# Moving some SBUF arrays of a decoder-layer kernel by 64 bytes, so that every operand of its large products starts at 32 modulo 128

## The chip, the cores and the metric

The kernel runs on one NeuronCore of one Trainium2 chip. The metric is the device time of one execution in microseconds, less is better. Its engines are TensorE (PE, with the load of its stationary operand shown apart as PEld), VectorE (DVE), ScalarE (ACT), GpSimd (POOL) and SyncE (SP), which here only issues transfers.

## The reference

One decoder layer for 512 prompt tokens and 64 sample tokens, all in float32 with D = 2048. What is computed, cut down:

```python
def mixer_block(x, ...):
    h = rmsnorm(x, w_norm_mix)
    proj = h @ w_in                                  # 2048 x 6160
    o_r, s_ret = retention_chunkwise(...)            # 4 heads
    o_g, s_gla = gla_chunked(...)                    # 4 heads
    mix = concat(norm(o_r) * silu(g_r), norm(o_g) * silu(g_g))
    return x + mix @ w_out, s_ret, s_gla

def peer_block(x, ...):                              # 16384 experts, 16 of them for each of 8 heads
    h = rmsnorm(x, w_norm_ffn)
    q = (h @ w_pq).reshape(T, 8, 2, 128)
    s1, s2 = q[:, :, 0] . sub_keys1, q[:, :, 1] . sub_keys2
    eidx, gate = top 16 of the sums of the two top 16, softmax
    act = gelu(sum(u_tab[eidx] * h))
    return x + sum(gate * act * v_tab[eidx])

y = rmsnorm(peer_block(mixer_block(x)))
```

## The kernel before

The 576 tokens lie in five tiles (`PTILES` = 4 of 128 prompt tokens, one of 64 sample tokens). Every large product is done at about float32 accuracy with three products of type `float32r`: each operand is split in a high part (rounded by an ACT copy) and a low part (the rest, a DVE subtraction), and TensorE adds high·high, high·low and low·high in a PSUM bank. One such product is one PEld (128x128 stationary) and one matmul (384 or 512 columns of the moving operand).

The stages follow one another, with a barrier of all engines between them:

1. **in_proj** (`project`, blocks 0 to 2 of the input projection), 0 to 197 us. Stationary: the token rows `own_hi`, `own_lo`. Moving: 512 columns of the weights. A block of weights is four buffers `q` = 0 to 3, of which `q` = 1 and 2 are `own.whi`, `own.wlo` (which the trace calls `whi`, `wlo`) and `q` = 0 and 3 are `in_proj_whi`, `in_proj_wlo`, the projection's own arrays.
2. **mixer** (`project_and_mix`), to 867 us: the other blocks of the projection from `own` and `whi`, `wlo` (products L1600 to L1603), interleaved with the retention and GLA heads, whose small products use `mixer_*` arrays.
3. **out_proj**, to 1100 us, and **queries**, to 1323 us: `project` again, four blocks each (products L612, L617, L618; L612 and L615 for the sample tile). In queries the rows of tiles 1 to 3 are `dense_hi`, `dense_lo` (the "dense tokens", 384 of them), those of tiles 0 and 4 are `queries_rows_hi`, `queries_rows_lo`. Block 0 goes tile by tile with transposes (L601) between, blocks 1 to 3 without.
4. **hidden** (`experts_hidden`), to 2542 us: 128 units `n`, one for each 128 rows of `u_tab`. A unit is 48 products, its stationary `un.hi`, `un.lo` (the buffers `whi`, `wlo`), its moving operand `dense_hi`, `dense_lo`:

```python
for x in range(KT):
    mm(o, un.hi[s][:, x, :], h_hi[:, x, :], start=x == 0, stop=False)
    mm(o, un.hi[s][:, x, :], h_lo[:, x, :], start=False, stop=False)
un.ready(pe, n)
for x in range(KT):
    ins = mm(o, un.lo[s][:, x, :], h_hi[:, x, :], start=False, stop=x == KT - 1)
```

   Between units TensorE does small float32 products: in units 1 to 63 the scores of the router (whose top-16 search is DVE work, `route`), from unit 64 on the gate matrices (`hidden_tq`, L2058, 4 matmuls each, two or four groups of them in a unit). `un.ready` waits for the low part of the unit. DVE also takes one dot product for each gathered row (L2300).
5. **outputs** (`outputs`), to 3630 us: 128 units of 48 products, stationary `whi`, `wlo`, moving `outputs_w_hi`, `outputs_w_lo` (L2557 to L2559). Then **finish**.

SBUF arrays are laid out as a stack: `sbuf_tensor` puts the next array behind the last one from the low end, and with `side="right"` before the last one from the high end. So each array's start follows from the sizes of those that were put down before it. Starts modulo 128 bytes of the operands of the large products, worked out from those sizes, with the same number for every slice that a product takes, as all steps are multiples of 128 bytes:

| array | role | before | after |
|---|---|---|---|
| `whi`, `wlo` (shared) | stationary in hidden and outputs, moving elsewhere | 32 | 32 |
| `own_hi`, `own_lo`, `out_proj_rows_*`, `queries_rows_*` | stationary | 32 | 32 |
| `out_proj_whi`, `queries_whi` and their `wlo` | moving | 32 | 32 |
| `outputs_w_hi`, `outputs_w_lo` | moving | 32 | 32 |
| `in_proj_whi`, `in_proj_wlo` (q = 0, 3) | moving | 96 | 32 |
| `dense_hi`, `dense_lo` | stationary in queries, moving in hidden | 96 | 32 |
| `mixer_qk`, `_v`, `_kd`, `_qkT`, `_qd`, `_at`, `_S`, `_qm`, `_km`, `_dec` | small products of the mixer | 96 | 32 |
| `mixer_wa2`, `mixer_alr` | small products of the mixer | 64 | 0 |

Of the kernel before, what the change touches and what calls it, by code (L numbers as in the profile page):

```python
# [26 lines left out]
F32 = mybir.dt.float32  # L27
# [6 lines left out]
P = 128  # L34
# [4 lines left out]
TILES = SEQ // P + 1  # L39
# [42 lines left out]
class Steps:  # L82


    def __init__(self, eng, sem):
        self.eng, self.sem, self.base, self.n, self.offset = eng, sem, 0, 0, 0
# [25 lines left out]
class Alloc:  # L112
# [12 lines left out]
    def sb(self, name, shape, dt=F32):  # L125
        return self.ctx.enter_context(self.nc.sbuf_tensor(f"{self.name}_{name}", shape, dt))
# [542 lines left out]
class InputRows:  # L669


    def __init__(self, a, sb, whi, wlo):
        self.hi, self.lo = (sb(f"own_{p}", [P, KT, cols], F32R) for p, cols in (("hi", TP), ("lo", SEQ)))
        self.whi, self.wlo = whi, wlo
        self.rstd = sb("own_rstd", [P, 16])[:, 0:TILES]
        self.raw_in = [a.sem(f"own_raw_in{s}") for s in range(2)]
        self.hi_done, self.lo_done = a.sem("own_hi_done"), a.sem("own_lo_done")

# [1981 lines left out]
def build(nc, x, w, consts, keys, tables, states, outs):  # L2660

    def scratch(name, shape):
        return nc.dram_tensor(name, shape, F32, kind="Internal").ap()

    proj, alr = scratch("proj", (TP, PROJ - 2 * H * DV)), scratch("alr", (RANK, SEQ + NSMP))
    normed = scratch("normed", (TP, D))
    mix, sums = scratch("mix", (TP, D)), scratch("sums", (TP, D))
    queries, h_rows = scratch("queries", (TP, D)), scratch("h_rows", (2, P, D))
    hidden, G = scratch("hidden", (NCH, P, CH, ND)), scratch("gate_mat", (NCH, P, NG, CH, GT))

    with ExitStack() as ctx:
        def sb(name, shape, dt=F32, on=ctx):
            return on.enter_context(nc.sbuf_tensor(name, shape, dt))

        ident, squares = sb("ident", [P, P]), sb("squares", [P, D // NB, TILES])
        rstd_all = sb("rstd_all", [P, 16])[:, 0:TILES]
        shared = Alloc(nc, ctx, "units")
        raw = [sb(f"raw{s}", [P, KT // KQ, NB]) for s in range(2)]
        whi, wlo = ([sb(f"{name}{s}", [P, KT // KQ, NB], F32R) for s in range(2)] for name in ("whi", "wlo"))
        un = Units(nc, shared, raw, whi, wlo)  # L2680
        with ExitStack() as early:
            tiles = [sb(f"x{s}", [P, D], F32, early) for s in range(2)]
            held, ahead = (Held(shared, name, raw, whi, wlo, tiles) for name in ("held", "ahead"))
            with ExitStack() as inputs:
                own = InputRows(shared, lambda name, shape, dt=F32: sb(name, shape, dt, inputs), whi, wlo)
                project(nc, "in_proj", ident, consts["ident"], x, w["in"], proj, w_col_dram=w["norm_mix"], late=True,
                        small=(w["alr"], alr), own=own, held=held)
                project_and_mix(nc, "mixer", consts, ident, own, held, w["in"], w["out"], proj, alr, w["a2"], w["gn"], states,
                                outs["states"], normed, mix)
            project(nc, "out_proj", ident, None, mix, w["out"], sums, squares=squares, residual=x, first=True, held=held,  # L2690
                    then=(ahead, w["pq"]), rstd_all=rstd_all)
            expert_ids, gates0, dots = (ctx.enter_context(nc.sbuf_tensor(name, [P, NGATHER], dt, side="right"))
                                        for name, dt in (("expert_ids", U32), ("gates0", F32), ("dots", F32)))
            rows = ctx.enter_context(ExitStack())
            dense = [rows.enter_context(nc.sbuf_tensor(f"dense_{p}", [P, KT, ND], F32R, side="right")) for p in ("hi", "lo")]
            project(nc, "queries", ident, None, sums, w["pq"], queries, w_col_dram=w["norm_ffn_cols"], squares=squares, row=h_rows,
                    dense=dense, first=True, held=ahead, rstd_all=rstd_all, un=un, u_units=tables["u_units"])
        with rows:
            big, w_in = [shared.sb(f"big{n}", [P, NKEYS * GT]) for n in range(2)], shared.sem("w_in")
            experts_hidden(nc, "hidden", consts, ident, un, big, w_in, tables["u_units"], tables["v_units"], *dense, hidden, queries, keys, tables["u_rows"], h_rows,  # L2700
                           w["norm_ffn"], expert_ids, dots, gates0, G)
        acc, accg = sb("acc", [P, KT, ND]), [sb(f"accg{x}", [P, D]) for x in range(2)]
        X, early = sb("sums1", [P, D]), shared.sem("sums_early")
        outputs(nc, "outputs", un, big, w_in, tables["v_units"], hidden, G, tables["v_rows"], expert_ids, dots, acc, accg, sums, X, early)
        finish(nc, "finish", ident, sums, w["norm_final"], acc, accg, X, outs["y"])
# [62 lines left out]
```

## Time and profile before

| | |
|---|---|
| median of 3 runs | 3663.56 us (3657.59 to 3664.55) |
| profiled execution | 3668.83 us, its span 3667.0 us |
| PE, DVE, ACT, POOL busy | 3528.2, 2585.5, 1314.1, 937.1 us |
| granted TensorE clock, mean | 0.984 |

The span is the time from the first to the last instruction in the profiled execution; busy is the time in which an engine worked. Matmuls overlap, so the duration of one (334 ns) says little of the rate: that is read from the distance between the starts of consecutive ones, called pitch below.

### The profile page before, as it was taken

How to read it: one execution, taken by the hardware profiler on the slowest of the kernel's cores; microseconds unless marked ns; L12 is line 12 of the kernel's file. 1: busy time of each engine (PE TensorE's matmuls, PEld its weight loads, DVE VectorE, ACT ScalarE, POOL GpSimd, SP SyncE). 2: the span in 40 equal slices, each digit the busy share in tenths (PEclk: the TensorE clock that was granted, in tenths of full speed). 3: DMA queues.
4: the chain of work that ended last, by engine and by line, in shares of the span. 5: the costliest groups of instructions: out<-in, count | busy, mean ns of one | idle time of the engine just before them, and what ended most of it. 6: DMA issues, size and time to landing. Idle time of an engine off the chain costs nothing. (4 is left out here: it accounts for less than half of the span.)

```text
span 3667.0 us, 50045 instructions
## 1 busy us (share of the span) xinstructions
PE 3528.2 (96%) x19463; PEld 3267.5 (89%) x19463; DVE 2585.5 (71%) x3886; ACT 1314.1 (36%) x1671; POOL 937.1 (26%) x619
## 2 busy tenths in 40 slices
PE   8999999998989999999999999998999999999996
PEld 6877777776867889999999999998999999999996
DVE  4135555553224238999998888886898898998997
ACT  5111134442223223332236767673222222222222
POOL 0000000000000000233333333331555554554552
PEclk9999999999999999999999999999999999999998
DMA  5145343435334244688789999998989999989896
GB/s 204 50 144 172 108 140 128 125 130 185 141 107 162 86 156 160 256 329 333 293 321 364 384 376 375 382 374 343 360 339 372 360 356 377 360 355 370 348 359 243
DMA packets 193659, 965.07 MB, mean 263 GB/s; under 512 B 19697, under 2 KB 67121, under 8 KB 92706
## 3 DMA queue, kind: packets, MB, share of 16 engines
q1 hardware_dynamic: 121010, 516.50, 37.9%
q0 software_dynamic: 61424, 426.27, 29.9%
q10 hardware_dynamic: 11008, 19.26, 1.5%
q8 instruction: 154, 2.52, 0.3%
q14 instruction: 63, 0.52, 0.0%
HBM read 865.58 MB, written 96.37 MB: 262 GB/s over the span
## 5 line engine op out<-in xcount | busy, mean ns | idle before, releaser
L2068 PE MATMUL hidden_hp<-dense_hi,whi 128*128 128x384 f32 x2048 | 699.8, 342 | 6.1 <-PEq L123 6.1
L1836 ACT CAST whi<-raw 128x2048 fp32r<-128x2048 f32 x214 | 410.7, 1919 | 790.5 <-PE outputs_vp L2559 599.9
L2069 PE MATMUL hidden_hp<-dense_lo,whi 128*128 128x384 f32 x2048 | 691.8, 338 | 0.0
L2557 PE MATMUL outputs_vp<-outputs_w_hi,whi 128*128 128x384 f32 x2032 | 679.6, 334 | 3.3 <-DVE wlo L1840 3.1
L2559 PE MATMUL outputs_vp<-outputs_w_hi,wlo 128*128 128x384 f32 x2032 | 678.8, 334 | 0.0
L2558 PE MATMUL outputs_vp<-outputs_w_lo,whi 128*128 128x384 f32 x2032 | 678.7, 334 | 0.0
L2015 POOL DMA_INDIRECT hidden_row<-u_rows,expert_ids x192 | 363.5, 1893 | 1000.4 <-DVE dots L2300 625.4
L1840 DVE TENSOR_TENSOR wlo<-raw,whi 128x2048 fp32r<-128x2048 f32 x214 | 490.2, 2291 | 105.0 <-ACT whi L1836 103.4
L2493 DVE SCALAR_TENSOR_TENSOR accg<-outputs_row,outputs_w_op,accg 128x2048 f32<-128x2048 f32 x192 | 450.7, 2347 | 54.8 <-DMA outputs_row<-v_rows,outputs_id 51.8
L2300 DVE CUSTOM_DVE_ANT_0 hidden_row<-hidden_row,hidden_h_row 128x2048 f32<-128x2048 f32 x192 | 436.0, 2287 | 67.7 <-DMA hidden_row<-u_rows,expert_ids 64.8
L2355 POOL DMA_INDIRECT outputs_row<-v_rows,outputs_id x192 | 325.6, 1696 | 522.3 <-DVE accg L2493 477.8
L2068 PEld LDWEIGHTS hidden_hp<-dense_hi,whi 128*128 128x128 f32 x2048 | 386.6, 189 | 6.5 <-issue 6.5
L2072 PE MATMUL hidden_hp<-dense_hi,wlo 128*128 128x384 f32 x2048 | 380.1, 337 | 12.7 <-DVE wlo L1840 12.5
L2557 PEld LDWEIGHTS outputs_vp<-outputs_w_hi,whi 128*128 128x128 f32 x2032 | 381.4, 188 | 5.6 <-DVE wlo L1840 5.6
L2069 PEld LDWEIGHTS hidden_hp<-dense_lo,whi 128*128 128x128 f32 x2048 | 386.2, 189 | 0.0
L2558 PEld LDWEIGHTS outputs_vp<-outputs_w_lo,whi 128*128 128x128 f32 x2032 | 381.4, 188 | 0.0
L2559 PEld LDWEIGHTS outputs_vp<-outputs_w_hi,wlo 128*128 128x128 f32 x2032 | 381.4, 188 | 0.0
L2072 PEld LDWEIGHTS hidden_hp<-dense_hi,wlo 128*128 128x128 f32 x2048 | 359.2, 188 | 15.9 <-DVE wlo L1840 15.9
L1600 PE MATMUL mixer_acc<-whi,own_hi 128*128 128x512 f32 x720 | 297.8, 414 | 7.1 <-PEq L123 7.1
L1601 PE MATMUL mixer_acc<-wlo,own_hi 128*128 128x512 f32 x720 | 284.6, 395 | 0.0
L2146 ACT ACTIVATE hidden_hid<-hidden_hp 128x384 f32<-128x384 f32 x128 | 62.8, 491 | 571.7 <-PE hidden_hp L2072 571.7
L2347 POOL COPY outputs_id<-expert_ids 128x1 uint32 (+1 forms) x192 | 220.3, 1148 | 37.1 <-POOLq L123 35.9
(397 smaller groups left out, 5032.6 us busy)
## 6 DMA issues: line engine op xcount, KB each, us to landing
raw<-v_units SPq DMA_DIRECT2D x128, 1024.0 KB
raw<-u_units SPq DMA_DIRECT2D x86, 1024.0 KB
raw<-w_in SPq DMA_DIRECT2D x42, 1024.0 KB, 5.8
hidden_raw<-u_units SPq DMA_DIRECT2D x42, 1024.0 KB
hidden<-hidden_hid SPq DMA_DIRECT2D x128, 192.0 KB
gate_mat<-units_big SPq DMA_DIRECT2D x12, 2048.0 KB, 20.0
units_big<-hidden SPq DMA_DIRECT2D x16, 1536.0 KB
units_big<-gate_mat SPq DMA_DIRECT2D x16, 1536.0 KB
```

Source lines behind the costliest of these rows:

```text
L1836: self.nc.scalar.copy(self.hi[s][:], self.raw[raw][:]).then_inc(self.hi_done, 1)
L1840: self.nc.vector.tensor_tensor(self.lo[s][:], self.raw[self.slot(n, s)][:], self.hi[s][:].bitcast(F32), ALU.subtract).then_inc(self.lo_don ...
L2015: pool.indirect_dma_start(row[g % U_ROWS][:], None, u_rows, bass.IndirectOffsetOnAxis(expert_ids[:, g:g + 1], 0)).then_inc(row_in[g % U_RO ...
L2068: mm(o, un.hi[s][:, x, :], h_hi[:, x, :], start=x == 0, stop=False)
L2069: mm(o, un.hi[s][:, x, :], h_lo[:, x, :], start=False, stop=False)
L2072: ins = mm(o, un.lo[s][:, x, :], h_hi[:, x, :], start=False, stop=x == KT - 1)
L2300: v.tensor_tensor_reduce(r[:], r[:], h_row[g % 3 // 2][:], 1.0, 0.0, mult, ALU.add, dots[:, g:g + 1]).then_inc(row_used, 1)
L2355: pool.indirect_dma_start(self.row[j % ROWS][:], None, self.table, bass.IndirectOffsetOnAxis(self.id[j][:], 0)).then_inc(self.row_in[j % R ...
L2493: v.scalar_tensor_tensor(o[:], r[:], w_op[:, j:j + 1], o[:], mult, ALU.add).then_inc(gat.row_used, 1)
L2557: mm(o, un.hi[x][:, at, :], W_hi[s][:, e, :], start=e == 0, stop=False)
L2558: mm(o, un.hi[x][:, at, :], W_lo[s][:, e, :], start=False, stop=False)
L2559: ins = mm(o, un.lo[x][:, at, :], W_hi[s][:, e, :], start=False, stop=e == CH - 1)
```

## The change

Two arrays of 64 bytes per partition are added, neither of which is read or written. `own_rstd` grows from 16 to 32 floats (five are used), which moves all that is put down behind it in the stages in_proj and mixer up by 64 bytes. `edge` is put down from the high end before `expert_ids`, `gates0`, `dots`, `dense_hi` and `dense_lo`, which moves these five down by 64 bytes. No instruction is added, removed or moved on any engine.

```diff
@@ InputRows.__init__ @@
         self.hi, self.lo = (sb(f"own_{p}", [P, KT, cols], F32R) for p, cols in (("hi", TP), ("lo", SEQ)))
         self.whi, self.wlo = whi, wlo
-        self.rstd = sb("own_rstd", [P, 16])[:, 0:TILES]
+        self.rstd = sb("own_rstd", [P, 32])[:, 0:TILES]
@@ build @@
             project(nc, "out_proj", ident, None, mix, w["out"], sums, squares=squares, residual=x, first=True, held=held,
                     then=(ahead, w["pq"]), rstd_all=rstd_all)
+            ctx.enter_context(nc.sbuf_tensor("edge", [P, 16], F32, side="right"))
             expert_ids, gates0, dots = (ctx.enter_context(nc.sbuf_tensor(name, [P, NGATHER], dt, side="right"))
```

## Rows read from the trace of the kernel before

**Rows 1.** Busy time of each engine by stretch: columns named in the first row
```profile
core 0: us, PE busy (x) PEld busy (x) DVE busy (x) ACT busy (x) POOL busy (x), PEclk, DMA share, GB/s
1493.00:1896.00 403.00, 390.32 (x2263) 386.81 (x2263) 386.32 (x841) 118.88 (x118) 138.77 (x68) 1.00 0.82 315
1981.00:2433.00 452.00, 450.28 (x2775) 449.21 (x2774) 379.94 (x530) 316.15 (x547) 163.35 (x90) 1.00 0.99 380
2720.00:3635.00 915.00, 910.99 (x5262) 909.06 (x5261) 820.19 (x634) 246.70 (x139) 462.50 (x320) 1.00 0.90 353
```

**Rows 2.** Waits of PE, 1493 to 1900 us: total us, times, longest
```profile
PE hidden_hp L2072 <- DVE wlo L1840: 12.5, 8, 2.4
```

**Rows 3.** Waits of PE, 1981 to 2433 us
```profile
PE hidden_tq L2058 <- DVE hidden_spare L2308: 1.6, 1, 1.6
```

**Rows 4.** Waits of DVE, 1493 to 1900 us
```profile
DVE hidden_row L2300 <- DMA hidden_row<-u_rows,expert_ids: 7.2, 5, 2.5
DVE wlo L1840 <- ACT whi L1836: 0.2, 1, 0.2
```

**Rows 5.** Timeline of PE in outputs: start us, us, what
```profile
2999.77 0.33 PE L2557 MATMUL outputs_vp<-outputs_w_hi,whi 128*128 128x384 f32 x1
...
3002.89 0.33 PE L2557 MATMUL outputs_vp<-outputs_w_hi,whi 128*128 128x384 f32 x1
```

**Rows 6.** Timeline of PE in queries, block 2, tiles 0 and 1
```profile
1240.45 0.39 PE L612 MATMUL queries_acc<-queries_whi,queries_rows_hi 128*128 128x512 f32 x1
...
1243.17 0.39 PE L612 MATMUL queries_acc<-queries_whi,dense_hi 128*128 128x512 f32 x1
...
1249.35 0.39 PE L612 MATMUL queries_acc<-queries_whi,dense_hi 128*128 128x512 f32 x1
```

**Rows 7.** Timeline of PE in in_proj: `in_proj_whi`, then `whi`
```profile
80.35 0.39 PE L612 MATMUL in_proj_acc<-in_proj_whi,own_hi 128*128 128x512 f32 x1
...
85.84 0.39 PE L612 MATMUL in_proj_acc<-in_proj_whi,own_hi 128*128 128x512 f32 x1
...
109.98 0.39 PE L612 MATMUL in_proj_acc<-whi,own_hi 128*128 128x512 f32 x1
...
112.02 0.39 PE L612 MATMUL in_proj_acc<-whi,own_hi 128*128 128x512 f32 x1
```

**Rows 8.** Timeline of PE in hidden: the 16 last products of five units
```profile
1840.91 2.94 PE L2072 MATMUL hidden_hp<-dense_hi,wlo 128*128 128x384 f32 x16
...
1997.92 2.99 PE L2072 MATMUL hidden_hp<-dense_hi,wlo 128*128 128x384 f32 x16
...
2428.32 2.99 PE L2072 MATMUL hidden_hp<-dense_hi,wlo 128*128 128x384 f32 x16
...
2496.92 2.96 PE L2072 MATMUL hidden_hp<-dense_hi,wlo 128*128 128x384 f32 x16
...
2530.45 2.96 PE L2072 MATMUL hidden_hp<-dense_hi,wlo 128*128 128x384 f32 x16
```

**Rows 9.** Timeline of PE, units 67 and 100 of hidden: start, end of each
```profile
1942.80 0.42 PE L2068 MATMUL hidden_hp<-dense_hi,whi 128*128 128x384 f32 x1
...
1951.20 1.05 PE L2058 MATMUL hidden_tq<-hidden_spare 128*128 128x128 f32 x8
...
2272.94 0.42 PE L2068 MATMUL hidden_hp<-dense_hi,whi 128*128 128x384 f32 x1
...
2281.51 1.95 PE L2058 MATMUL hidden_tq<-hidden_spare 128*128 128x128 f32 x16
```

**Rows 10.** Timeline of PE in outputs behind two waits
```profile
2718.39 0.44 PE L2557 MATMUL outputs_vp<-outputs_w_hi,whi 128*128 128x384 f32 x1 [2.08 <-DVE wlo L1840]
...
2720.24 0.33 PE L2558 MATMUL outputs_vp<-outputs_w_lo,whi 128*128 128x384 f32 x1
...
2852.99 0.45 PE L2557 MATMUL outputs_vp<-outputs_w_hi,whi 128*128 128x384 f32 x1
...
2854.86 0.33 PE L2558 MATMUL outputs_vp<-outputs_w_lo,whi 128*128 128x384 f32 x1
```

**Rows 11.** Timeline of DVE around 2196 us: a gathered row that came late
```profile
2196.26 2.29 DVE L2300 CUSTOM_DVE_ANT_0 hidden_row<-hidden_row,hidden_h_row 128x2048 f32<-128x2048 f32 x1 [4.80 <-DMA hidden_row<-u_rows,expert_ids]
```

## The prediction, made before the changed kernel was run

> **What bounds the kernel now.** I read the stretches first, then the waits of PE and of DVE, then PE's timeline in each stage, looking at the pitch of consecutive products. The reader is to see in the stretches that PE is busy nearly all the time in every part but one. From 1981 to 2433 us it is busy 450.3 of 452 us, in outputs 911.0 of 915 us [rows 1]. There the pitch of the products is the time. The exception is 1493 to 1896 us, where the router runs. PE waits there eight times, 12.5 us in all, for the low part that DVE makes [rows 2]. DVE itself is busy 386.3 of 403 us [rows 1], and of the rest it waits 7.2 us for gathered rows and only 0.2 us for anything that hangs on PE [rows 4]. In that stretch DVE with its gathers sets the pace.
>
> So the question is whether the pitch depends on where the operands lie. This trace holds both cases.
>
> - **512 columns.** In queries, 12 pitches with the stationary operand in `queries_rows_*` (32 modulo 128) take 1243.17 − 1240.45 = 2.72 us, 226.7 ns each. At 1243.17 us the stationary goes over to `dense_*` (96), while the moving operand, the shape and the loop stay. The next 27 take 1249.35 − 1243.17 = 6.18 us, 228.9 ns each [rows 6]. In in_proj, 24 pitches with the moving operand at 96 take 5.49 us, 228.8 ns each, and 9 with it at 32 take 2.04 us, 226.7 ns [rows 7]. A pair that lies apart by 64 costs 2.2 ns more, whichever of the two it is.
> - **384 columns.** In outputs all lie at 32, and 18 pitches take 3.12 us, 173.3 ns each [rows 5]. In hidden, where the moving operand is at 96, units come in three kinds, told apart by the row of their 16 last products: 2.94, 2.96 or 2.99 us [rows 8]. Fifteen pitches lie in such a row, and the last matmul is some 0.335 to 0.34 us. So the pitches are about 173.3, 174.7 and 176.7 ns. A unit keeps its kind from its start to its end.
>
> **The change part by part.** No instruction changes, so all rests on the pitch, and on what else could depend on a start.
>
> *Hidden, 1981 to 2433 us.* Here 38 of the 44 units from 72 to 115 are of the 2.99 kind, the first and the last of them at 1997.92 and 2428.32 us [rows 8]. Unit 100 is one: its 48 pitches, from its first product to the first gate product behind it, take 2281.51 − 2272.94 = 8.57 us [rows 9]. 48 at 173.3 ns are 8.32 us. The 0.25 us above has two parts: the other pitches are 3.4 ns too long, 0.15 us, and 0.10 us are the restart. An aligned unit would not reach 8.32 us either, since it starts behind the gate products too. Two restarts in outputs show what aligned operands cost there: 10 pitches take 1.85 and 1.87 us in place of 1.733, that is 0.117 and 0.137 us more, after which the pitch is at 173.3 ns again [rows 10]. I take 0.125 us. The gain is 0.25 − 0.125 = 0.125 us for a unit, for 38 of them 4.75 us. Bounds: 0.113 and 0.133 us by the two restarts, so 4.3 to 5.1 us; nothing if the pitch hangs on something else.
>
> *Hidden, the other units behind the router.* The last six units follow one another without a restart and are of the 2.96 kind. The rows of five of them stand 2530.45 − 2496.92 = 33.53 us apart, 8.38 us for a unit against 8.32 [rows 8], so they give 0.4 us. About 15 more, of the 2.94 and 2.96 kinds, start behind gate products. Unit 67, of the first kind, takes 1951.20 − 1942.80 = 8.40 us [rows 9], 0.08 us above 8.32; the other kind has 1.3 ns more in each pitch, so 0.14 us. They lie on both sides of the aligned 0.125. Together I put −0.1 us on them. That makes 5.0 us.
>
> *Hidden, under the router.* Until 1896 us the gain of PE turns into a longer wait for DVE. I take 0 for 1493 to 1896 us, and 0.3 us for the units before, of which two are of the slowest kind. If all passed through, the some 45 units would give about 1.5 us: that is the upper end.
>
> *Queries.* Blocks 1 to 3 hold 3 x 3 tiles x 48 = 432 products on `dense_*` at 2.2 ns: 1.0 us. In block 0 every 12 products are interrupted by transposes, and the start costs as much as the pitch would give; I take 0.
>
> *In_proj.* Blocks 1 and 2 hold 2 x 2 buffers x (4 tiles x 12 + 8) = 224 products on `in_proj_whi`, `in_proj_wlo`: 0.5 us.
>
> *Mixer.* The large products keep their operands at 32. The small ones move from 96 to 32, and restart the large ones as before. No row shows a pair of them in both places. I take 0, with 1.5 us on either side: a hundred or so restarts with at most 10 to 15 ns, half the spread between the restarts in outputs [rows 10].
>
> *Outputs, finish.* No operand moves. They start earlier by what is gained before, since a barrier stands ahead of each stage. DVE, ACT and transfers keep their lengths: a start goes from 96 to 32 modulo 128, or from 64 to 0, and no row gives one of them another length for that.
>
> The sum is 4.75 + 0.25 + 0.3 + 1.0 + 0.5 = 6.8 us. The profiled execution took 3668.8 us (span 3667.0), so it would take 3662.0. Against the median of the runs, 5.3 us below it, the same difference gives 3663.6 − 6.8 = **3656.8 us**.
>
> **A rule that speaks against the change.** The rows of queries show two pitches for two places of one operand, with all else equal [rows 6]. The Trainium skill, "TensorE: Matmul & The Clock Gate", section "Step-by-step: what each phase is for", says that TensorE has two independent SBUF read ports, one for the streaming operand and one for the weight load, so that loading the next weights takes no read bandwidth from the running matmul. By that rule where the two lie to each other would not matter, and the sum would be 0 in place of 6.8 us. It is the first rival below.
>
> **The rivals.**
>
> - *The place isn't the cause: the pitch hangs on how a run of products starts.* For it: in hidden units of all three kinds read the very same arrays [rows 8], so the place alone can't set the kind; the phase at the restart must have a part. Against it: in queries the pitch changes at 1243.17 us in the middle of a run, with no restart [rows 6], and both restarts in outputs come back to 173.3 ns [rows 10]. If it holds, the units may fall into other kinds, and nothing is gained on the whole: 3663.6 us, give or take 3.
> - *The pitch falls, but the stretch behind it absorbs the gain.* From 1981 to 2433 us the DMA engines are busy at a share of 0.99 [rows 1]. For it: one row came 4.8 us late there [rows 11], and PE waited 1.6 us for DVE behind it [rows 3]. Against it: that is PE's only wait in 452 us, and in the fastest units the same share was no hindrance. Then only queries, in_proj and the last units are left: 1.0 + 0.5 + 0.4 + 0.3 = 2.2 us, so 3661.4 us.
> - *More is gained:* part of the 1.5 us under the router, the mixer's 1.5 us, and restarts as good as the best in hidden (0.08 us in place of 0.125, 38 x 0.045 = 1.7 us). 6.8 + 4.4 = 11.2 us: 3652.4 us.
> - *Slower: gathered rows come late more often.* A unit shorter by 1.2% asks for 1.2% more transfers per us, of engines that are busy at 0.99. Each late row like that in [rows 11] costs PE 1.6 us [rows 3]. It decides once there are more than four of them beside the present one, which eats the 6.8 us; with ten, the time is 3663.6 − 6.8 + 16 = 3672.8 us. Against it: every such wait also gives the transfers time to catch up, so the rate would settle where PE no longer gains, not beyond.
>
> **How the numbers follow.** A measurement of this kernel tells apart some 0.2%, 7.3 us: its three runs lie within 7 us. My forecast (gain of 4.5 to 9 us, 3654.5 to 3659) gets 0.53. No effect of the place gets 0.18, the absorbed gain 0.10, the larger gain 0.13, slower 0.06. The forecast lies just inside 7.3 us, so of its 0.53 I give 0.22 to faster; with the 0.13 and some 0.03 of the no-effect case faster is 0.38. Slower is 0.06 and 0.01 of no-effect, the rest, 0.55, is within 0.2%. The range reaches from the larger gain to no effect: 3652 to 3664 us.
>
> **What would show it.** Right: the rows of 16 products in hidden from 1981 us on are 2.93 to 2.94 us, none of 2.99; the pitch on `dense_*` in queries and on `in_proj_whi` is 226.7 ns; the stretch of units 72 to 115 is shorter by 4 to 5 us; 1493 to 1896 us keeps its length, with more of PE's wait on `wlo`; outputs keeps its own. Wrong: rows of 2.96 and 2.99 us with all operands at 32, PE waits on L2308 or on `whi` behind late transfers from 1981 us on, or a mixer that is longer by more than 2 us.

## The result and the profile after: 3675.6 us, slower by 0.28%

| | before | after |
|---|---|---|
| median (lowest to highest) | 3664.06 us of 10 runs (3657.59 to 3669.15) | 3675.64 us of 10 runs (3668.26 to 3677.64) |
| ratio, 95% interval | | 1.0028 [1.0019, 1.0038] |
| profiled execution, its span | 3668.83, 3667.0 us | 3675.49, 3673.7 us |
| PE busy | 3528.2 us | 3537.8 us |

The forecast was 3656.8 us, with a range of 3652 to 3664, so a kernel that is 6.8 us faster. It became slower by 7 to 14 us.

From the page of the changed kernel, PE's busy time and the three groups of hidden (busy us, mean ns of one):

```profile
PE 3537.8 (96%) x19463; PEld 3274.5 (89%) x19463; DVE 2585.6 (70%) x3886; ACT 1314.1 (36%) x1671; POOL 963.9 (26%) x619
...
L2068 PE MATMUL hidden_hp<-dense_hi,whi 128*128 128x384 f32 x2048 | 701.5, 343 | 6.1 <-PEq L123 6.1
L2069 PE MATMUL hidden_hp<-dense_lo,whi 128*128 128x384 f32 x2048 | 693.6, 339 | 0.0
...
L2072 PE MATMUL hidden_hp<-dense_hi,wlo 128*128 128x384 f32 x2048 | 382.1, 338 | 9.6 <-DVE wlo L1840 9.5
```

The same lines of before have 699.8, 691.8 and 380.1 us. DVE and ACT, whose operands moved too, are as busy as they were. The products themselves became longer. The stretches of the changed kernel, which answer to [rows 1]:

```profile
core 0: us, PE busy (x) PEld busy (x) DVE busy (x) ACT busy (x) POOL busy (x), PEclk, DMA share, GB/s
1493.00:1896.00 403.00, 394.52 (x2270) 391.63 (x2269) 385.42 (x838) 123.00 (x123) 137.05 (x67) 1.00 0.83 317
1981.00:2433.00 452.00, 451.16 (x2784) 450.86 (x2783) 383.46 (x529) 317.37 (x550) 172.40 (x92) 1.00 0.99 381
2720.00:3635.00 915.00, 910.70 (x5242) 908.01 (x5240) 820.66 (x630) 243.03 (x135) 474.86 (x322) 1.00 0.90 354
```

PE's waits in 1493 to 1900 us of the changed kernel, as in [rows 2] (us in total, times, longest):

```profile
PE hidden_hp L2072 <- DVE wlo L1840: 8.4, 7, 1.9
```

and in 1981 to 2433 us, as in [rows 3]:

```profile
PE hidden_tq L2058 <- DVE hidden_spare L2308: 0.8, 1, 0.8
```

Under the router PE waits 4.1 us less than in [rows 2] and is busy 4.2 us more: longer products use up a wait, they don't lengthen the stretch. Behind it nothing is late. So the pitch has to be looked at. PE in queries, block 2: a pair with `queries_rows_*`, the first one with `dense_*`, and the one behind the last (start us, us), as in [rows 6]:

```profile
1246.16 0.39 PE L617 MATMUL queries_acc<-queries_wlo,queries_rows_hi 128*128 128x512 f32 x1
...
1248.43 0.40 PE L618 MATMUL queries_acc<-queries_whi,queries_rows_lo 128*128 128x512 f32 x1
1248.66 0.40 PE L612 MATMUL queries_acc<-queries_whi,dense_hi 128*128 128x512 f32 x1
...
1257.03 0.39 PE L612 MATMUL queries_acc<-queries_whi,queries_rows_hi 128*128 128x512 f32 x1
```

10 pitches with `queries_rows_*` take 2.27 us, 227 ns each. The 36 with `dense_*` take 8.37 us, **232.5 ns** each, where before had 228.9. Both arrays, `queries_rows_*` and `dense_*`, now start at 32 modulo 128. In in_proj 24 pitches on `in_proj_whi`, `in_proj_wlo` take 5.60 us, 233.3 ns, where [rows 7] have 228.8:

```profile
80.01 0.39 PE L612 MATMUL in_proj_acc<-in_proj_whi,own_hi 128*128 128x512 f32 x1
...
85.61 0.39 PE L612 MATMUL in_proj_acc<-in_proj_whi,own_hi 128*128 128x512 f32 x1
```

In hidden, rows of 16 last products as in [rows 8]:

```profile
1984.60 2.98 PE L2072 MATMUL hidden_hp<-dense_hi,wlo 128*128 128x384 f32 x16
...
2224.12 2.98 PE L2072 MATMUL hidden_hp<-dense_hi,wlo 128*128 128x384 f32 x16
...
2535.51 2.98 PE L2072 MATMUL hidden_hp<-dense_hi,wlo 128*128 128x384 f32 x16
```

All rows of 16 from 1981 to 2433 us, 45 of them, say 2.98: a pitch of some 176 ns, between the second and the third kind of before. No unit is of the 2.94 kind any more. Outputs, whose operands didn't move, has 18 pitches in 3.12 us, as in [rows 5]:

```profile
2999.59 0.33 PE L2557 MATMUL outputs_vp<-outputs_w_hi,whi 128*128 128x384 f32 x1
...
3002.71 0.33 PE L2557 MATMUL outputs_vp<-outputs_w_hi,whi 128*128 128x384 f32 x1
```

### The profile page after: what moved, and what is told of

The parts are those of the page before. It is cut to its first block and busy times, and to the rows that moved or that the text cites. A ratio compares the mean times of both kernels' runs of the same rounds, so it can differ in the third digit from the quotient of the medians.

```text
span 3673.7 us, 50045 instructions
## 1 busy us (share of the span) xinstructions
PE 3537.8 (96%) x19463; PEld 3274.5 (89%) x19463; DVE 2585.6 (70%) x3886; ACT 1314.1 (36%) x1671; POOL 963.9 (26%) x619
## 5 line engine op out<-in xcount | busy, mean ns | idle before, releaser
L2068 PE MATMUL hidden_hp<-dense_hi,whi 128*128 128x384 f32 x2048 | 701.5, 343 | 6.1 <-PEq L123 6.1
L2069 PE MATMUL hidden_hp<-dense_lo,whi 128*128 128x384 f32 x2048 | 693.6, 339 | 0.0
L2015 POOL DMA_INDIRECT hidden_row<-u_rows,expert_ids x192 | 377.2, 1965 | 990.2 <-DVE dots L2300 602.4
L2068 PEld LDWEIGHTS hidden_hp<-dense_hi,whi 128*128 128x128 f32 x2048 | 386.4, 189 | 6.5 <-issue 6.5
L2072 PE MATMUL hidden_hp<-dense_hi,wlo 128*128 128x384 f32 x2048 | 382.1, 338 | 9.6 <-DVE wlo L1840 9.5
L2069 PEld LDWEIGHTS hidden_hp<-dense_lo,whi 128*128 128x128 f32 x2048 | 386.5, 189 | 0.0
L2072 PEld LDWEIGHTS hidden_hp<-dense_hi,wlo 128*128 128x128 f32 x2048 | 361.3, 188 | 12.5 <-DVE wlo L1840 12.5
L2347 POOL COPY outputs_id<-expert_ids 128x1 uint32 (+1 forms) x192 | 228.2, 1189 | 34.1 <-POOLq L123 32.9
```

The lines of the kernel that those rows point to most:

```text
L2015: pool.indirect_dma_start(row[g % U_ROWS][:], None, u_rows, bass.IndirectOffsetOnAxis(expert_ids[:, g:g + 1], 0)).then_inc(row_in[g % U_RO ...
```

## What the table of starts had left out

The table ahead of the prediction goes by 128 bytes. Worked out modulo 256 from the same sizes, the starts are:

| array | before | after |
|---|---|---|
| `whi`, `wlo`, `own_*`, `queries_rows_*`, `queries_whi`, `out_proj_*`, `outputs_w_*` | 32 | 32 |
| `in_proj_whi`, `in_proj_wlo` | 96 | 160 |
| `dense_hi`, `dense_lo` | 224 | 160 |

So 64 bytes carried each of the moved arrays not onto the others, but to the opposite side of a circle of 256. Below, *d* is the start of the moving operand less that of the stationary one, modulo 256. In queries and in_proj (512 columns) d was 64 and became 128. In hidden (384 columns), where `dense_*` is the moving operand, it was 192 and became 128. Outputs and out_proj have 0. In in_proj *d* follows from the size of `own_rstd` alone; in queries it also hangs on where the low and the high end of the memory lie. The table below checks this: at equal *d* the two stages agree within 0.7 ns in every kernel.

**Theory A:** the pitch hangs on d, it is shortest at 0, and 128 is worse than 64. **Rival B:** the absolute start counts (32 modulo 256 is the good one, 160 a bad one). **Rival C:** the places don't matter, and the kinds of the units are drawn anew in each execution. **Rival D:** something else that was moved (small products of the mixer, gathers, DVE) costs the time.

## The experiments

The edits are to the kernel before. `own_rstd` sets the place of `in_proj_w*` and the mixer's arrays, `edge` that of `dense_*`. All kernels compute all of the reference. `before` ran again beside each, and the ratios are to these runs: median 3665.29 us (29 runs, 3657.2 to 3675.78) beside all_256, all_256_up and edge_only, 3666.58 us (23 runs) beside rstd_only and after_again. A kernel of which there is one run has only its pitches to show, as single runs of before lie up to 19 us apart.

Means over whole stages, from the starts of all consecutive products (queries blocks 1 to 3 on `dense_*`; in_proj blocks 1 and 2 on `in_proj_w*`; hidden without waits and restarts), in ns:

| kernel | d in queries, in_proj, hidden | queries | in_proj | hidden |
|---|---|---|---|---|
| before | 64, 64, 192 | 229.0 | 229.0 | 175.0 |
| the same, again | 64, 64, 192 | 229.0 | 229.0 | 174.3 |
| after | 128, 128, 128 | 232.4 | 233.1 | 175.9 |
| the same, again | 128, 128, 128 | 232.4 | 232.9 | 175.9 |
| edge_only | 128, 64, 128 | 232.4 | 229.0 | 175.9 |
| rstd_only | 64, 128, 192 | 229.0 | 232.9 | 174.2 |
| all_256 | 0, 0, 0 | 226.7 | 226.8 | 173.4 |
| all_256_up | 0, 0, 0 | 226.7 | 226.8 | 173.4 |
| dist_96 | 96, 96, 160 | 233.4 | 233.4 | 173.3 |
| dist_160 | 160, 160, 96 | 234.2 | 234.3 | 176.6 |
| dist_192 | 192, 192, 64 | 233.4 | 233.3 | 173.3 |
| dist_224 | 224, 224, 32 | 233.2 | 233.3 | 174.1 |
| dist_320 | 64, 64, 192 | 229.0 | 229.1 | 174.3 |

Lengths of stages, from first product to first product, in us (the mixer, in_proj, out_proj and queries to their last product):

| stage | before | again | after | again | all_256 |
|---|---|---|---|---|---|
| in_proj | 181.10 | 181.04 | 181.94 | 181.97 | 180.40 |
| mixer | 646.18 | 643.31 | 649.48 | 641.72 | 646.85 |
| out_proj | 212.14 | 212.15 | 212.09 | 212.67 | 212.08 |
| queries | 216.53 | 216.67 | 218.45 | 219.56 | 215.60 |
| hidden, units 0 to 17 | 170.18 | 170.16 | 171.58 | 171.72 | 169.73 |
| 18 to 62 (router) | 402.78 | 404.67 | 402.90 | 403.35 | 403.71 |
| 63 to 71 | 95.86 | 92.33 | 94.34 | 95.84 | 94.57 |
| 72 to 115 | 440.93 | 433.72 | 438.83 | 437.76 | 434.22 |
| 116 to 126 | 100.16 | 101.03 | 101.04 | 101.05 | 99.66 |

### All operands at one place modulo 256

```diff
-        self.rstd = sb("own_rstd", [P, 16])[:, 0:TILES]
+        self.rstd = sb("own_rstd", [P, 64])[:, 0:TILES]
...
+            ctx.enter_context(nc.sbuf_tensor("edge", [P, 48], F32, side="right"))
```

> own_rstd has 64 floats and edge 48, so the moving and the stationary operand of every large product start a multiple of 256 bytes apart (in the change of this case they are 128 apart for in_proj_whi and dense, before they were 64 apart). Theory A (the distance of the two starts modulo 256 sets the pitch: 0 is best, 64 costs some, 128 most): pitch 226.7 ns on in_proj_whi and on dense_* in queries, 173.3 ns in hidden with rows of 16 products of 2.93 to 2.94 us, time some 5 to 9 us below the kernel before, ratio about 0.998. Theory B (the start of each operand modulo 128 sets it, 32 is good or bad): nothing differs from the changed kernel, pitch 232 ns in queries, ratio about 1.003. Theory C (the phase at a restart sets it, the place has no part): the pitch falls anyhow, between 226.7 and 233, with no order.

Measured 3660.33 us (3656.35 to 3664.98, 12 runs), ratio to before 0.9985 [0.9975, 0.9995]. PE in queries, block 2, from the first product on `dense_*` to the one behind the last:

```profile
1243.03 0.39 PE L612 MATMUL queries_acc<-queries_whi,dense_hi 128*128 128x512 f32 x1
...
1251.19 0.39 PE L612 MATMUL queries_acc<-queries_whi,queries_rows_hi 128*128 128x512 f32 x1
```

36 pitches in 8.16 us, 226.7 ns: the step at the change of the array is gone. In hidden:

```profile
1996.38 2.93 PE L2072 MATMUL hidden_hp<-dense_hi,wlo 128*128 128x384 f32 x16
...
2223.89 2.93 PE L2072 MATMUL hidden_hp<-dense_hi,wlo 128*128 128x384 f32 x16
...
2530.17 2.94 PE L2072 MATMUL hidden_hp<-dense_hi,wlo 128*128 128x384 f32 x16
```

All 45 rows of 16 from 1981 to 2433 us say 2.93 or 2.94. The changed kernel's operands are at the same place modulo 128 as these. It is the 256 that tells them apart, and rival C falls: with d = 0 the draw between kinds is gone.

The next one shifts everything up by 64 bytes, so that all large operands lie at 96 modulo 256:

```diff
+        sb("low_pad", [P, 16])
         raw = [sb(f"raw{s}", [P, KT // KQ, NB]) for s in range(2)]
...
-        self.rstd = sb("own_rstd", [P, 16])[:, 0:TILES]
+        self.rstd = sb("own_rstd", [P, 64])[:, 0:TILES]
...
+            ctx.enter_context(nc.sbuf_tensor("edge", [P, 32], F32, side="right"))
```

> As all_256, but all operands of the large products lie 64 bytes higher, at 96 modulo 128 (a pad of 16 floats below raw, edge 32 floats), with the same distances. Theory A: pitches and time as in all_256, 226.7 and 173.3 ns. Theory B (a start at 96 is worse than one at 32, or a good place modulo 256 of each operand by itself): pitches differ from all_256 in out_proj and outputs too, where all operands have moved off 32.

Measured 3660.06 us (3654.9 to 3665.49), ratio 0.9983 [0.9972, 0.9994], and the same pitches in all three stages. So at d = 0 the absolute start has no part, and rival B falls. Other distances were not run with everything shifted.

### Each half of the change alone

```diff
+            ctx.enter_context(nc.sbuf_tensor("edge", [P, 16], F32, side="right"))
```

> Only the second half of the change: edge of 16 floats, so that dense_* lies 128 from the stationary or moving partner; in_proj_whi stays 64 away. Theory A: queries at 232.3 ns and hidden at 176 ns as in the changed kernel, in_proj at 229 ns as before. Time: if the loss is in queries and hidden, most of the changed kernel's +0.28% is here, about 1.002; if it is in the mixer's small products or in clock events of the mixer, about 1.0005.

Measured 3670.62 us (3667.02 to 3674.52), ratio 1.0012 [1.0001, 1.0022]. Queries and hidden have the changed kernel's pitches, in_proj those of before. The interval of the ratio holds both values that were expected, 1.002 and 1.0005, so it is the pitches that say where the loss lies.

```diff
-        self.rstd = sb("own_rstd", [P, 16])[:, 0:TILES]
+        self.rstd = sb("own_rstd", [P, 32])[:, 0:TILES]
```

> Only the first half of the change: own_rstd of 32 floats, so that in_proj_whi and the mixer's small operands lie 128 from own_* and whi; dense_* stays where it was before. Theory A: in_proj at 233 ns, 0.9 us longer than before; queries and hidden as before. If the mixer's small operands matter too, the mixer is about 2 us longer at the same number of half-clock intervals; ratio about 1.001. If the mixer has no part, 1.0003.

Measured 3668.05 us (3661.42 to 3673.59), ratio 1.0008 [0.9998, 1.0017]. In_proj has 232.9 ns and lasts 181.96 us, 0.9 longer than before, and the rest has the pitches of before. Its mixer, whose small operands all moved, takes 643.29 us, the same as the 643.31 us of the second profile of before. Both have 22.2 us at half the clock of TensorE there (on this see below), so the places of the small operands cost nothing that can be seen. By the ratios `edge` costs some 4 us and `own_rstd` some 3, each with an interval of 3 to 4 us to either side. Only 0.9 of the latter has a place in the profile, and its interval takes in 0.9 us. Rival D isn't needed.

### Both kernels once more

No edit; a second profile of each.

> The kernel before once more, for a second profile: its first one took 3668.8 us, near the top of its ten runs (3657.6 to 3669.2). All theories: same pitches as in the first profile in queries (229) and in_proj (229); if hidden's three kinds of units come from the phase at restarts, their counts may differ; clock events and the mixer's length show how much of the 6.7 us between the two first profiles is no effect of the change.

Measured 3658.48 us, one run, 10 us below the profile on which the prediction was made. Its hidden, the same kernel as in [rows 8]:

```profile
1983.33 2.94 PE L2072 MATMUL hidden_hp<-dense_hi,wlo 128*128 128x384 f32 x16
1993.47 2.96 PE L2072 MATMUL hidden_hp<-dense_hi,wlo 128*128 128x384 f32 x16
...
2229.82 2.96 PE L2072 MATMUL hidden_hp<-dense_hi,wlo 128*128 128x384 f32 x16
...
2528.20 2.99 PE L2072 MATMUL hidden_hp<-dense_hi,wlo 128*128 128x384 f32 x16
```

From 1981 to 2433 us it has 23 rows of 2.94, 23 of 2.96 and none of 2.99, where the first profile had 4, 3 and 38. Units 72 to 115 take 433.72 us against 440.93. Of these 7.2 us the pitch is 44 units x 47 x (176.39 − 173.95 ns) = 5.0 us, the rest lies between units, where the first profile has the wait of [rows 3]. The addresses are the same in both. So with d = 192 the kind of a unit is drawn at run time, and the draw alone moves this stretch by 5 us. In the four profiles with this distance in hidden (both of before, rstd_only, dist_320) 43, 15, 6 and 8 of the 128 units are of the slowest kind: the prediction was made on the most unlucky of them.

> The changed kernel once more, beside rstd_only on the same chip. Theory A: ratio near 1.0028, hidden at 176 ns with no unit at 173.3, as in its first profile, since two starts 128 apart have no good phase to fall into.

Measured 3673.03 us (3667.2 to 3679.3), ratio 1.0018 [1.0008, 1.0027]: slower again, by less. Its pitches are those of the first profile. Its mixer takes 641.72 us, 7.8 less than in the first. There the two executions differ in one more thing, the clock of TensorE. Two stretches of the first profile of the changed kernel (column before the DMA share: granted clock):

```profile
core 0: us, PE busy (x) PEld busy (x) DVE busy (x) ACT busy (x) POOL busy (x), PEclk, DMA share, GB/s
223.60:227.00 3.40, 3.40 (x10) 2.64 (x9) 2.02 (x1) 1.35 (x1) 0.00 (x0) 0.51 0.99 323
626.40:629.80 3.40, 3.40 (x11) 2.66 (x10) 3.07 (x7) 1.54 (x3) 0.54 (x1) 0.50 0.43 89
```

The same two stretches of the second profile:

```profile
223.60:227.00 3.40, 3.40 (x17) 2.81 (x16) 2.29 (x1) 0.55 (x1) 0.00 (x0) 1.00 0.85 318
626.40:629.80 3.40, 3.40 (x16) 2.64 (x17) 1.57 (x3) 0.00 (x0) 0.00 (x0) 1.00 0.67 246
```

TensorE was granted 1.2 of its 2.4 GHz in the first profile there and 2.4 in the second. Added up over the mixer, from its first product to its last, the first profile has 31.7 us at half clock and the second 19.7. Work that fills 12 us at half clock takes 6 us at full, so by this estimate the clock explains some 6 of the 7.8 us. The profiles of all kernels agree: the mixer's length goes with its time at half clock, from 641.7 us with 19.7 to 649.4 us with 34.0, some 0.55 us for each us at half clock and within 1 us of that line in all 14, wherever its small operands lie. So the mixer's +3.3 us in the first profile after, with 3.4 us more at half clock, are no effect of the places.

### Other distances

Sizes of `own_rstd` and `edge` in floats: 24 and 8, 40 and 24, 48 and 32, 56 and 40, 80 and 64 for dist_96, dist_160, dist_192, dist_224 and dist_320. One of them, the others alike:

```diff
-        self.rstd = sb("own_rstd", [P, 16])[:, 0:TILES]
+        self.rstd = sb("own_rstd", [P, 24])[:, 0:TILES]
...
+            ctx.enter_context(nc.sbuf_tensor("edge", [P, 8], F32, side="right"))
```

> Map of the distance: in_proj_whi 96 above, dense_* 96 below its partner modulo 256. Theory A: a pitch between that at 64 (229.0 ns) and at 128 (232 to 233 ns) in in_proj and queries.

> Map of the distance: 192 bytes, that is 64 the other way round. Theory A with distances counted round a circle of 256: 229.0 ns, as at 64, and hidden with units of several kinds. Rival: the pitch grows with the distance up to just below 256: over 233 ns.

Measured 3667.6 and 3664.49 us, one run each. Block 2 of queries and a unit of hidden, first of dist_96:

```profile
1247.32 0.39 PE L612 MATMUL queries_acc<-queries_whi,dense_hi 128*128 128x512 f32 x1
...
1255.72 0.40 PE L612 MATMUL queries_acc<-queries_whi,queries_rows_hi 128*128 128x512 f32 x1
...
1992.02 2.94 PE L2072 MATMUL hidden_hp<-dense_hi,wlo 128*128 128x384 f32 x16
```

then of dist_192:

```profile
1247.73 0.40 PE L612 MATMUL queries_acc<-queries_whi,dense_hi 128*128 128x512 f32 x1
...
1256.12 0.39 PE L612 MATMUL queries_acc<-queries_whi,queries_rows_hi 128*128 128x512 f32 x1
...
1990.57 2.94 PE L2072 MATMUL hidden_hp<-dense_hi,wlo 128*128 128x384 f32 x16
```

Queries needs 8.40 and 8.39 us for its 36 pitches, 233.3 ns. Hidden has the shortest pitch in both. At d = 96 queries lies above the 232.4 ns of 128 and not between 64 and 128, as was expected: a miss. That d = 192 costs as much as 96 in queries, and not the 229.0 ns of 64, was a miss: I had taken the distance as that on a circle, the same to either side. Which of the two operands lies ahead counts.

> Distance of 320 bytes, the 64 of the kernel before and 256 more, in in_proj and for dense_*. If the pitch has a period of 256 bytes: 229.0 ns in in_proj and queries, with the same order 229, 231.7, 225.9 of the three pitches in queries, and hidden with units of several kinds between 173.3 and 176.7 ns. If the period is longer: other numbers.

Measured 3662.64 us, one run, beside 3663.01 of before on the same chip.

```profile
1245.73 0.39 PE L612 MATMUL queries_acc<-queries_whi,dense_hi 128*128 128x512 f32 x1
...
1253.97 0.39 PE L612 MATMUL queries_acc<-queries_whi,queries_rows_hi 128*128 128x512 f32 x1
...
1989.04 2.96 PE L2072 MATMUL hidden_hp<-dense_hi,wlo 128*128 128x384 f32 x16
1999.17 2.94 PE L2072 MATMUL hidden_hp<-dense_hi,wlo 128*128 128x384 f32 x16
```

36 pitches in 8.24 us, 228.9 ns, as at 64, and hidden is mixed of the kinds of before. The arrays moved by 256 from their places in before, and no pitch changed, while 128 bytes more (all_256 beside the changed kernel) changed all three: the period is 256.

> Map of the distance, after dist_192 gave 233.4 ns in queries and in_proj but 173.3 in hidden: with the sign counted (stationary minus moving, modulo 256) this is -160 in in_proj and queries, +160 in hidden. Theory: still high, 232 to 234 ns, in queries and in_proj, as at -96, -128 and -192; hidden is at -96 counted the other way, open.

> Map of the distance: stationary minus moving is -224, that is +32, in in_proj and queries and -32 in hidden. Theory: between +64 (233.4) and 0 (226.7) in queries and in_proj; hidden near 173.3, as at its neighbours 0 and -64.

Measured 3678.15 and 3665.68 us, one run each. From dist_160:

```profile
1251.63 0.39 PE L612 MATMUL queries_acc<-queries_whi,dense_hi 128*128 128x512 f32 x1
...
1260.06 0.40 PE L612 MATMUL queries_acc<-queries_whi,queries_rows_hi 128*128 128x512 f32 x1
...
1997.93 2.99 PE L2072 MATMUL hidden_hp<-dense_hi,wlo 128*128 128x384 f32 x16
```

8.43 us, 234.2 ns: the longest of all, and all its units are of the 2.99 kind. It is also the slowest kernel, 15 us above before on the same chip, with one run each; its mixer has the most time at half clock, 34.0 us. dist_224 has 233.2 ns in queries and a mixed hidden, 98 units at 173.3 ns and 27 at 176.5 or more, where 173.3 was expected for all.

The distance isn't all that counts. At the same d = 64 queries (512 columns) is 2.3 ns above its shortest pitch and hidden (384 columns) at its shortest; at 160 it is 7.5 ns and nothing.

### Which of the pairs collides

A product's weights are loaded while the one before it runs, so two pairs could matter: a product's own two operands, or the moving operand and the weights that are loaded meanwhile. Here `dense_hi` keeps d = 0 and `dense_lo` has 128:

```diff
# all_256, and
             dense = []
             for p in ("hi", "lo"):
+                if p == "lo":
+                    rows.enter_context(nc.sbuf_tensor("between", [P, 32], F32, side="right"))
                 dense.append(rows.enter_context(nc.sbuf_tensor(f"dense_{p}", [P, KT, ND], F32R, side="right")))
```

> As all_256, but with 128 bytes between dense_hi and dense_lo, so that dense_lo alone lies 128 from its partner. If the running matmul's moving operand and the weight load of the next product collide: in queries the pitch behind L617 (during which dense_lo is loaded for L618) is long, 232 ns or more, and that behind L612 is 226.7; in hidden, where whi is always loaded, the pitch behind L2069 (dense_lo moving) is long, 176 ns, the one behind L2068 short, 173.3, and L2072 (dense_hi alone) 173.3. If a product's own two operands collide, it is the same in hidden, but in queries the pitch behind L618 is the long one.

Measured 3663.44 us, one run. In queries, block 2:

```profile
1240.48 0.39 PE L612 MATMUL queries_acc<-queries_whi,dense_hi 128*128 128x512 f32 x1
1240.70 0.40 PE L617 MATMUL queries_acc<-queries_wlo,dense_hi 128*128 128x512 f32 x1
1240.94 0.40 PE L618 MATMUL queries_acc<-queries_whi,dense_lo 128*128 128x512 f32 x1
1241.17 0.39 PE L612 MATMUL queries_acc<-queries_whi,dense_hi 128*128 128x512 f32 x1
```

Rows are rounded to 10 ns, so the means over all blocks say more: L612 to L617 226.7 ns, L617 to L618 232.6, L618 to L612 234.1. The first is as short as with d = 0 for all: both products have `dense_hi`, and no address of `dense_lo` is in play. The second is long although L617 itself has d = 0: what is loaded during it is `dense_lo`. That fits a clash of the load with the running product. The third doesn't: `dense_hi`, which is loaded during L618, is at d = 0, and only L618's own weights are at 128. So the expectation was half met. A rule of load against running product explains the second pitch and not the third, one of a product's own operands the third and not the second. Nor does hidden fit: both rules gave 173.3 ns behind L2068, 176 behind L2069 and 173.3 behind L2072, and in units 72 to 115 it is 174.6, 175.4 and 173.6. The weight loads of queries, blocks 1 to 3 (busy us, mean ns of one), two lines of lo_apart and one of all_256:

```profile
L612 PEld LDWEIGHTS queries_acc<-queries_whi,dense_hi 128*128 128x128 f32 x71 | 13.6, 192 | 3.1
L618 PEld LDWEIGHTS queries_acc<-queries_whi,dense_lo 128*128 128x128 f32 x71 | 13.3, 188 | 2.8
...
L612 PEld LDWEIGHTS queries_acc<-queries_whi,dense_hi 128*128 128x128 f32 x70 | 13.1, 188 | 2.7
```

The load of `dense_lo`, which falls in the second pitch, is no longer than any other; it is the load of `dense_hi` in the third that takes 192 ns and not 188. What the mechanism is stays open.

## Why the prediction was wrong, point by point

- **The pitch depends on where the operands lie: right.** The two pitches of queries in [rows 6], 226.7 and 228.9 ns, came again in before_again and dist_320, and the step at the change of the array goes away with d = 0. The first rival has one pitch for all places, and it falls for 512 columns: the place alone takes the pitch from 226.7 to 234.2 ns. It holds in part for hidden, where at d = 192 the kind of a unit is drawn anew in each execution. The Trainium skill, "TensorE: Matmul & The Clock Gate", section "Step-by-step: what each phase is for", says that two independent read ports keep the weight load from taking bandwidth from the running matmul. By that rule the places of the two would not matter, and the runs don't agree with that: in lo_apart even the pitch that starts with L617, whose own two operands are at d = 0, is 5.9 ns longer.
- **"A pair that lies apart by 64 costs 2.2 ns more", and so 32 modulo 128 for all is aligned: this step failed.** The trace held the distances 0 and 64, and 192 in hidden. I worked out the starts modulo 128 and took "the same modulo 128" for "together". No row of before had a pair that is 128 apart, so the sum rested on a case that the trace doesn't show. It costs 3.4 to 4.1 ns more than 64, not 2.2 less. My lower bound, "nothing if the pitch hangs on something else", left out a longer pitch, which no row excluded, and the range should have had it.
- **Queries 1.0, in_proj 0.5, early units 0.3 us less.** They became 1.9, 0.8 and 1.4 us more. With d = 0 they are 0.9, 0.7 and 0.45 us less: the sizes were about right, for another change.
- **38 units of the 2.99 kind, 4.75 us: this failed too.** The count was one execution's draw, and the sum took it off the median of the runs, 5.3 us below that execution. By the second profile of before it would have been none in this stretch. Against the first profile the changed kernel's units 72 to 115 are 2.1 us shorter (pitch 176.0 ns against 176.4), against the second 5.1 us longer (174.0 ns there). The profiled execution of before, 3668.83 us, is near the top of its runs, 3669.15, and the second, 3658.48, near their bottom, 3657.59. The cost of a restart was mis-sized as well: with d = 0 the first pitches behind the gate products lie 3.67 us above 173.3 ns in these 44 units, 0.083 us each and not the 0.125 us taken from outputs. So 38 x (0.25 − 0.083) = 6.3 us, where all_256 is 6.7 us shorter than that execution.
- **The stretch under the router keeps its length: right.** 402.90 us against 402.78, in all five profiles 402.8 to 404.7. The sign was turned: PE's wait for `wlo` fell from 12.5 to 8.4 us.
- **Late gathered rows: not seen.** PE's waits from 1981 to 2433 us fell to 0.8 us. The kernel is slower for another reason than that rival's.
- **The mixer at 0: right, as far as can be seen.** Its length moved by 7.8 us between two executions of one kernel, but with the clock: rstd_only and the second profile of before, with 22.2 us at half clock each, have 643.29 and 643.31 us.
- **The whole.** Against the second profile of before the changed kernel has, in us: in_proj +0.9, queries +1.8, units 0 to 17 +1.4, router −1.8, 63 to 71 +2.0, 72 to 115 +5.1. That is 9.4, and the ratios of the two sets of runs give 6.6 and 10.3. The −1.8 and the +2.0 belong together: an interval of 3.4 us at half clock, worth 1.7 us, lies under the router in the second profile of before, and in units 63 to 71 in the changed kernel. The mixer's +6.2 us, with 9.5 us more at half clock, is left out.

The two kernels with d = 0 are faster than both: 3660.3 and 3660.1 us, 5 to 6 us below before. It is about what was forecast for this change, and that is in part luck: against the second profile of before, all_256 gains nothing in units 72 to 115 (434.22 us against 433.72), where 4.75 of the 6.8 us were to come from.

## What to carry to other kernels

Before shifting an array to align it, work out the distance of both operands of a product at a period larger than the one you believe in, and list which distances the trace really holds; a place that no row shows has a price on both sides. Run the neighbours (the pad and three times the pad): here 64 bytes lost 0.28% (0.18% in the second set of runs) and 192 bytes gained 0.15%. And where instructions come in kinds that the address doesn't tell apart, take a second profile before a count of them goes into a sum.

## What the runs showed that I had not expected

- The pitch of back-to-back products depends on d with a period of 256 bytes and with a sign (at 96, 160, 192 and 224 with 512 columns, and at 32, 64, 96 and 160 with 384, from one profile each): with 512 columns 226.7 ns at 0, 229.0 at 64, 233.4 at 96, 232.4 to 233.1 at 128, 234.2 at 160, 233.4 at 192, 233.2 at 224. With 384 columns it is 173.3 or 173.4 at 0, 64 and 160, 176.6 at 96, 175.9 at 128, and mixed at 32 and 192.
- At mixed distances a unit of 48 products keeps one of three pitches (173.3, some 174.6, 176.7 ns) from its start to its end, and executions of the same kernel differ in how many have which: 43 or 15 of 128 above 176 ns. At d = 32 two of the three were seen.
- The pitch can stay long behind a run of a bad pair. In block 2 of queries the 20 products behind those on `dense_*`, which have d = 0, take 226.7 ns each in before, but 229.1 in dist_96, 228.1 in dist_192 and 227.8 in dist_160.
- Half-clock intervals of 3.4 us come and go in the mixer between executions of one kernel, and its length goes with them: 31.7 us of them and 649.5 us, or 19.7 and 641.7.
